# The last hidden group's down projection as seven block products for two output tiles at a time

## The chip, the cores and the metric

One program runs on one core of a Trainium2 chip. The metric is the device time of one execution in microseconds (us); lower is better. TensorE is called PE below, VectorE DVE, ScalarE ACT, GpSimd POOL; the queue on SyncE (SP) loads the weights.

## The reference

The reference is one step of a two-layer encoder trunk on 640 tokens (512 of a prompt, 8 streams of 16), width 1024, hidden width 2816, all in fp32:

```python
def half_swiglu(x, g, w_gu, w_down):
    h = rmsnorm(x, g) @ w_gu
    a, b = jnp.split(h, 2, axis=-1)
    return x + 0.5 * ((jax.nn.silu(a) * b) @ w_down)
...
def ple_add(x, p_i, g, w_gate, w_proj):
    gate = jax.nn.sigmoid((rmsnorm(x, g) @ w_gate).astype(F32))
    return x + (gate * (p_i @ w_proj).astype(F32)).astype(x.dtype)
```

Each layer is half_swiglu, a token mixer, half_swiglu, ple_add. The mixer is retention in layer 0 and stick-breaking attention in layer 1. So the eight phases are ffn, ret, ffn, ple, ffn, sb, ffn, ple, and each of the four ffn phases is followed by another phase that begins with an RMSNorm.

## The kernel before

x is kept transposed: 8 tiles x[:, d, :] of 128 features by 640 tokens. Every fp32 product is made of three passes in the reduced type fp32r: an operand is split into a high part (ACT copies it, names ending in _hi) and a low part (DVE subtracts, _lo), and PE multiplies hi*hi, hi*lo and lo*hi. The engines have one hand-written instruction order each and meet on counting semaphores; an engine waits at the head of its queue.

The weights come as a stream of slots. SP loads slot n into ring buffer raw[n % 4] as soon as the low part of slot n-4 has been made. In plain code ACT makes w_hi (split_hi, L1083) and DVE w_lo (split_lo, L1724), two slots ahead.

An ffn phase works the 22 hidden tiles in four groups, PIECES = (4, 6, 6, 6). Each group has its gate and up projection and then its down projection, which adds into x. Groups 1 to 3 do gate and up by a seven-product scheme over two-by-two blocks (winograd, product, L615) where plain blocks need eight. SEVEN_DOWN names the groups whose down projection also does that. There a job, d, makes two output tiles, d["out"] and d["out"] + 1, in 7 products of 9 matmuls (3 blocks, 3 passes, 320 columns): 63 matmuls. PE's order in such a job is product 1, product 3 of the job before, 2, 6, product 4 of the job before, 5, 7. The other engines serve it:

- ACT: snap1 (a copy within PSUM after product 1, L1184, needed by product 2), hi12 of the next job (L1147), snap2 (after product 6, needed by 7), hi34 (L1179, after the old job's product 4), hi56 and hi7 of the next job (L1167, L1173).
- DVE: c22 of the old job (L1856, needed by its product 4), lo56 (L1838, needed by product 6), lo7 (L1844), c11_c12 (L1873 and L1877, adds three quarters of the two tiles into x), the sums s1_s2 and s3 of the next job's weights (L1803 to L1809), c21 (L1883, the last quarter, which gives the PSUM banks free), lo12 of the next job (L1821), s4 (L1816) and lo34 (L1849).

The last group's down projection is plain before: for each of the 8 output tiles PE does 6 blocks in 3 passes over 2 halves, 36 matmuls (project, L544). After each tile, DVE adds it into x (L2052) and the next phase's operand is formed at once: ACT x_hi (feed_hi, L1087), ACT the square of x (square, L1094), DVE x_lo (feed_lo, L1729), POOL adds the square to ssum (add_squares, L1594 for the first, L1597 for the other seven). Two squares fit in the buffer, so square d waits for add d-2.

The next phase multiplies from the raw x and the gain and applies 1/rms afterwards. It begins so: ret runs its first projection (48 matmuls, q0) and then sum_squares (L567), which waits for all eight adds; sb does the same (its q0 starts only when the last down tile has left PSUM); ple runs three 12-matmul products of the small input p first (p_hi, p_lo, made during the down projection) and then sum_squares. p's fourth product waits for mean_square, the DVE reading of the sum. POOL issues the constants' DMAs of ret and sb after its last add.

Of the kernel before, what the change touches and what calls it, by code (L numbers as in the profile page):

```python
# [26 lines left out]
P = 128  # L27
D = 1024
KT = D // P
SEQ, STREAMS, STEP = 512, 8, 16  # L30
TOK = SEQ + STREAMS * STEP
# [18 lines left out]
SEVEN_DOWN = (1, 2)  # L50
# [153 lines left out]
def trunk(nc, phases, xT, pT, gains, wst, ones_d, ident_d, negtri_d, cs_d, dec_d, rmask_d, smask_d, gpow_d,  # L204
# [6 lines left out]
    with ctx:  # L211
# [221 lines left out]

        def g_tile(buf, k):

            return buf[:, k * TOK:(k + 1) * TOK]
# [99 lines left out]
        def _(pe):  # L536
# [45 lines left out]
            def ffn(c):  # L582
# [123 lines left out]
                for nf_at, nf in enumerate(PIECES):  # L706
# [363 lines left out]
        def _(act):  # L1070
# [19 lines left out]
            def square(c_fed, norm, d, s, value):  # L1090

                act.wait_ge(s, CREDIT + value)
                act.wait_ge(s_ssum, CREDIT + c_fed + d - 1)
                nc.scalar.activation(sq[:, d % 2, :], x[:, d, :], ACT.Square).then_inc(s_sq, 1)  # L1094
# [20 lines left out]
            def ffn(c):  # L1115
# [109 lines left out]

                def winograd(piece):
                    for old, d, new in jobs_of(c, piece):
# [25 lines left out]
                        if made:  # L1253
                            ghi(made)
                        if d["kind"] == "gu":
                            snap3(d)
                        if new:
                            hi56(new)
                            hi7(new)
                        else:  # L1260
                            act.wait_ge(s_prod[5], CREDIT + d["q"] + 1)
                            split_hi(c, d["m"], 0, 0, c["fill"] + d["m"])
                    if piece == LAST:
                        silu(d)
                        split_hi(c, d["m"] + 1, 0, 0, c["fill"] + d["m"] + 2)
                        ghi(d)

                for nf_at, nf in enumerate(PIECES):
# [38 lines left out]
                    for d in range(KT):  # L1307
                        if nf_at < LAST and d >= KT - 2:
                            if d == KT - 2:
                                first = fast_pairs(c, nf_at + 1)[0]  # L1310
                                hi12(first)
                                hi7(first)
                                hi56(first)
                            continue
                        split_hi(c, m + d, 0, 0, c["fill"] + m + d + 1)
                        if nf_at == LAST:
                            feed(c["fed"] + KT, c["norm"] + 1, d, s_free, o + m + d + 1)
                            if c["split_p"] and d == 4:
                                act.wait_ge(s_p, 16 * (c["ple"] + 1))
                                nc.scalar.activation(p_hi[:], p_raw[:], ACT.Copy).then_inc(s_phi, 1)  # L1320
# [263 lines left out]
        def _(pool):  # L1584
# [3 lines left out]
            def add_squares(fed, norm):  # L1588

                for d in range(KT - (norm == len(plan))):  # L1590
                    pool.wait_ge(s_sq, CREDIT + fed + d + 1)
                    if d == 0:
                        pool.wait_ge(s_ss, CREDIT + norm)
                        nc.gpsimd.tensor_copy(ssum[:], sq[:, 0, :]).then_inc(s_ssum, 1)  # L1594
                    else:
                        pool.wait_ge(s_ssum, CREDIT + fed + d)
                        nc.gpsimd.tensor_tensor(ssum[:], ssum[:], sq[:, d % 2, :], ALU.add).then_inc(s_ssum, 1)  # L1597
# [112 lines left out]
        def _(dve):  # L1710
# [46 lines left out]
            def ffn(c):  # L1757
# [177 lines left out]
                def winograd(piece):  # L1935
                    for old, d, new in jobs_of(c, piece):
# [20 lines left out]
                        if summed:  # L1957
                            c11_c12(summed)
                            s1_s2(new)
                            s3(new)  # L1960
                            c21(summed)
                            lo12(new)
                            s4(new)
                            lo34(d)
                            continue
# [20 lines left out]
                    if piece == LAST:  # L1986
                        c22(d)
                        split_lo(c, d["m"], 0, 0)
                        c12(d)
                        gated(d, 1)  # L1990
                        gated(d, 0)
                        split_lo(c, d["m"] + 1, 0, 0)
                        glo(d)

                for nf_at, nf in enumerate(PIECES):
# [52 lines left out]
                    for d in range(KT):  # L2048
# [4 lines left out]
                        if nf_at == LAST or d < KT - 2:  # L2053
# [3 lines left out]
                        if nf_at == LAST:  # L2057
                            feed_lo(c["fed"] + KT, c["norm"] + 1, d)
                            if c["split_p"] and d == 4:
                                dve.wait_ge(s_phi, CREDIT + c["ple"] + 1)  # L2060
                                tt(p_lo[:], p_raw[:], p_hi[:].bitcast(F), ALU.subtract).then_inc(s_plo, 1)
                        elif d == KT - 4:
# [597 lines left out]
```

## Time and profile before

| | us |
|---|---|
| median of three runs | 2795.7 |
| lowest and highest | 2793.03, 2796.23 |
| the profiled execution, its own time | 2792.98 |
| its span in the trace | 2791.4 |
| PE busy in the span | 2745.6 |
| DVE busy | 1918.0 |
| ACT busy | 1205.5 |

PE is busy nearly all the time; the other three matter only where PE has to wait for them. A time such as 308 ns of a matmul overlaps its neighbours; the distance from one matmul's start to the next is what counts.

### The profile page before, as it was taken

The page shows a single profiled execution, that of the slowest core. Times are in us where ns is not written, and L with a number is a line of the kernel's source. Part 1 is how long each engine was busy: PE and PEld are TensorE (multiplying, and loading weights), DVE is VectorE, ACT ScalarE, POOL GpSimd, SP SyncE. Part 2 cuts the span into 40 slices and gives each one's busy share as a digit, 9 for nine tenths or more (in the row PEclk, how much of TensorE's full clock was granted, in tenths as well). Part 3 has the DMA queues.
Part 4 walks back from the last instruction along what each step waited for, and adds up shares of the span by engine and source line. Part 5 has one row for each costly group of instructions (what it writes and reads, how often), then busy time and mean ns, then how long its engine had stood idle before and what let it go on. Part 6 is the DMA issues. An engine that isn't in the chain of part 4 may idle for free.

```text
span 2791.4 us, 47466 instructions
## 1 busy us (share of the span) xinstructions
PE 2745.6 (98%) x18946; PEld 2698.7 (97%) x18946; DVE 1918.0 (69%) x2687; ACT 1205.5 (43%) x1625; POOL 191.1 (7%) x190
## 2 busy tenths in 40 slices
PE   8999999999999999999999999999999999999997
PEld 8999999999999999999999999999999999999997
DVE  7788864646364677888657788864555567888755
ACT  5454443323232444454444454444434443545443
POOL 0000003101011110000010000002000020000021
PEclk9999999999999999999999999999999999999998
DMA  3322323333233313223321222323222112232231
GB/s 120 91 81 85 97 76 126 102 111 110 94 108 98 101 57 95 85 81 93 93 76 57 88 76 89 93 78 119 94 83 90 68 59 68 82 94 83 86 95 57
DMA packets 80908, 246.96 MB, mean 88 GB/s; under 512 B 8464, under 2 KB 25120, under 8 KB 79680
## 3 DMA queue, kind: packets, MB, share of 16 engines
q1 hardware_dynamic: 71408, 204.67, 23.5%
q0 software_dynamic: 9296, 39.40, 4.0%
q8 instruction: 149, 2.44, 0.4%
q14 instruction: 55, 0.45, 0.1%
HBM read 226.74 MB, written 17.30 MB: 87 GB/s over the span
## 4 chain that ended last, share of the span: by engine, by line
PE 94%; DVE 4%; ACT 1%; issue 1%; DMA 0%; ACTq 0%; SPq 0%; DVEq 0%
PE ps L615 42%; PE ps L544 32%; PE ps L927 7%; PE ps L803 4%; PE ps L980 2%; PE ps L596 1%; PE ps L901 1%; PE ps L1014 1%; DVE xn L1763 1%; PE ps L964 1%; PE ps L868 1%; PE ps L852 0%; PE ps L1000 0%; DVE w_lo L1724 0%; PE ps L871 0%
## 5 line engine op out<-in xcount | busy, mean ns | idle before, releaser
L1083 ACT ACTIVATE w_hi<-raw 128x1024 fp32r<-128x1024 f32 (+2 forms) x210 | 201.3, 959 | 516.6 <-PE ps L544 376.8
L1724 DVE TENSOR_TENSOR w_lo<-raw,w_hi 128x1024 fp32r<-128x1024 f32 (+2 forms) x210 | 236.8, 1128 | 93.9 <-ACT w_hi L1083 91.1
L544 PE MATMUL ps<-x_hi,w_hi 128*128 128x320 f32 x1216 | 284.3, 315 | 14.4 <-DVE x_lo L1729 8.9
L544 PE MATMUL ps<-x_lo,w_hi 128*128 128x320 f32 x1216 | 277.5, 309 | 0.0
L544 PE MATMUL ps<-x_hi,w_lo 128*128 128x320 f32 x1216 | 277.5, 310 | 0.0
L544 PEld LDWEIGHTS ps<-x_hi,w_hi 128*128 128x128 f32 x1216 | 203.9, 188 | 19.8 <-DVE w_lo L2466 8.9
L1147 ACT ACTIVATE wx_hi<-raw 128x1024 fp32r<-128x1024 f32 (+1 forms) x96 | 96.6, 1006 | 258.4 <-PE ps L615 226.2
L544 PEld LDWEIGHTS ps<-x_lo,w_hi 128*128 128x128 f32 x1216 | 203.8, 188 | 0.0
L544 PEld LDWEIGHTS ps<-x_hi,w_lo 128*128 128x128 f32 x1216 | 203.8, 188 | 0.0
L615 PE MATMUL ps<-x_hi,wx_hi 128*128 128x320 f32 x576 | 178.2, 309 | 3.0 <-DVE wx_lo L1821 3.0
L615 PE MATMUL ps<-x_hi,w_hi 128*128 128x320 f32 x576 | 178.7, 310 | 0.0
L615 PE MATMUL ps<-x_hi,w_lo 128*128 128x320 f32 x576 | 178.0, 309 | 0.0
L615 PE MATMUL ps<-x_lo,wx_hi 128*128 128x320 f32 x576 | 177.8, 309 | 0.0
L615 PE MATMUL ps<-x_lo,w_hi 128*128 128x320 f32 x576 | 177.6, 308 | 0.0
L615 PE MATMUL ps<-x_hi,wx_lo 128*128 128x320 f32 x576 | 177.5, 308 | 0.0
L615 PE MATMUL ps<-t_hi,w_lo 128*128 128x320 f32 x576 | 177.1, 307 | 0.0
L615 PE MATMUL ps<-t_lo,w_hi 128*128 128x320 f32 x576 | 177.1, 307 | 0.0
L615 PE MATMUL ps<-t_hi,w_hi 128*128 128x320 f32 x576 | 177.0, 307 | 0.0
L1821 DVE TENSOR_TENSOR wx_lo<-raw,wx_hi 128x1024 fp32r<-128x1024 f32 (+1 forms) x96 | 110.9, 1155 | 57.8 <-ACT wx_hi L1147 57.5
L544 PE MATMUL ps<-g_hi,w_hi 128*128 128x320 f32 x640 | 145.8, 308 | 0.0
L544 PE MATMUL ps<-g_hi,w_lo 128*128 128x320 f32 x640 | 145.5, 308 | 0.0
L544 PE MATMUL ps<-g_lo,w_hi 128*128 128x320 f32 x640 | 145.4, 308 | 0.0
(310 smaller groups left out, 7696.8 us busy)
## 6 DMA issues: line engine op xcount, KB each, us to landing
raw<-wst SPq DMA_DIRECT2D x292, 512.0 KB, 3.6
raw<-wst SPq DMA_DIRECT2D x96, 384.0 KB, 3.2
raw<-wst SPq DMA_DIRECT2D x32, 256.0 KB, 2.6
s<-st_d POOLq DMA_DIRECT2D x8, 1024.0 KB, 5.1
sts_o<-s POOLq DMA_DIRECT2D x16, 512.0 KB, 3.4
rd<-dec_d POOLq DMA_DIRECT2D x8, 640.0 KB, 5.6
kc<-kc_d POOLq DMA_DIRECT2D x8, 512.0 KB, 4.4
vc<-vc_d POOLq DMA_DIRECT2D x8, 512.0 KB, 5.2
```

The costliest lines, as they stand in the source:

```text
L544: last = nc.tensor.matmul(out[:, h, :], a, b[:, HALF * h:HALF * (h + 1)], start=start and q == 0, stop=stop and q == 2, skip_group_check=True)
L596: last = nc.tensor.matmul(acc(u)[:, h, :], a[:, p, w], b[:, k, cols], start=n in (0, 2) and k % 4 == 0 and q == 0, stop=n in (1, 3) and k ...
L615: last = nc.tensor.matmul(out, a[:, w], b[:, k, :], start=start and k == 0 and q == 0, stop=k == end - 1 and q == 2, skip_group_check=True)
L803: last = nc.tensor.matmul(out, a, b[:, p, w], start=part == 0 and k == 0 and q == 0 and t % 2 == 0, stop=part == 1 and k == 3 and q == 2, ...
L868: last = nc.tensor.matmul(f[:, t * DV:(t + 1) * DV], sc[:, t, :], vn[:, t, :], start=True, stop=t == 0)
L901: return nc.tensor.matmul(z[:, z0:z0 + w], bk[rows, par, b * P:(b + 1) * P], bq[rows, par, b * P:end], start=start, stop=False, skip_group ...
L927: last = nc.tensor.matmul(ps[:, sb_banks(use)[0], 0:HALF], a, b[:, xb, cols], start=n == 0 and q == 0, stop=n == len(blocks) - 1 and q == 2)
L980: last = nc.tensor.matmul(z[:, z0 + P * (b2 - b):z0 + ZW[b]], tri[:, int(b2 > b), :], src[:, from_piece, from_col:from_col + ZW[b2]], star ...
L1083: nc.scalar.activation(w_hi[:, (c["n"] + m) % 2, 0:cols], raw[:, r, 0:cols], ACT.Copy).then_inc(s_whi, 1)
L1147: nc.scalar.activation(wx_hi[:, 0:2, 0:d["width"]], raw_blocks(c, d)[:, 0:4:3, :], ACT.Copy).then_inc(s_hi12, 1)
L1724: tt(w_lo[:, p, 0:cols], raw[:, r, 0:cols], w_hi[:, p, 0:cols].bitcast(F), ALU.subtract).then_inc(s_wlo, 1)
L1821: tt(wx_lo[:, 0:2, w], raw_blocks(c, d)[:, 0:4:3, :], wx_hi[:, 0:2, w].bitcast(F), ALU.subtract).then_inc(s_lo12, 1)
```

## The change

The last group joins SEVEN_DOWN. Its down projection is then 4 jobs of 63 matmuls. The next phase's operand is formed two tiles at a time, in the middle of the following job (ACT fed, DVE two feed_lo). The squares come later: 0 and 1 in the third job, 2 to 4 at the end of the fourth, 5 to 7 after all of x_hi. The square buffers move to where the scheme's t_lo lies, since g_lo is in use to the end. Before a ple phase, the splitting of p sits in the third job. The gate values of the last group are formed with the extra sums of the seven-product layout (g_sum, ghi, glo), as in groups 1 and 2. Loads and slots keep their number and order.

```diff
--- before.py
+++ after.py
@@ -47,7 +47,7 @@
-SEVEN_DOWN = (1, 2)
+SEVEN_DOWN = (1, 2, 3)
...
@@ -251,6 +251,12 @@
+        with ExitStack() as s:
+
+            sb("over_t_hi2", [P, 3, 4, HALF], F, s)
+            sq_mix = sb("sq_mix", [P, 2, TOK], F, s)
+            sb("over_t_mid", [P, 3 * 4 * HALF - 4 * TOK], F, s)
+            sq_ple = sb("sq_ple", [P, 2, TOK], F, s)
...
@@ -471,7 +483,7 @@
-            nxt = fast_pairs(c, piece + 1)[0] if piece in SEVEN_DOWN else None
+            nxt = fast_pairs(c, piece + 1)[0] if piece < LAST else None
...
@@ -742,14 +754,6 @@
-                    if nf_at != LAST:
-                        m += KT
-                        continue
-                    with pe.Fori(0, KT // 4) as i:
-                        for j in range(4):
-                            step(m + j, i, 4)
-                            project(c, m + j, i, 4, (c["unit"] + 1 + m + j) % 4, [(k, k) for k in range(nf)],
-                                    tiles(g_hi), tiles(g_lo), ready if j == 0 else None)
...
@@ -1222,6 +1226,16 @@
+                def fed(d):
+
+                    act.wait_ge(s_up, CREDIT + 2 * d["sum"] + 2)
+                    feed_hi(c["norm"] + 1, d["out"])
+                    act.wait_ge(s_free, CREDIT + o + d["m"] + 2)
+                    feed_hi(c["norm"] + 1, d["out"] + 1)
+
+                def square_of(n):
+                    square(c["fed"] + KT, c["norm"] + 1, n, s_xhi, c["fed"] + KT + n + 1)
...
@@ -1252,6 +1266,14 @@
+                        if piece == LAST and d["kind"] == "dn":
+                            fed(old)
+                            if d["out"] == 4:
+                                square_of(0)
+                                square_of(1)
+                                if c["split_p"]:
+                                    act.wait_ge(s_p, 16 * (c["ple"] + 1))
+                                    nc.scalar.activation(p_hi[:], p_raw[:], ACT.Copy).then_inc(s_phi, 1)
...
@@ -1260,10 +1282,13 @@
                             split_hi(c, d["m"], 0, 0, c["fill"] + d["m"])
+                            for n in range(2, 5):
+                                square_of(n)
                     if piece == LAST:
-                        silu(d)
                         split_hi(c, d["m"] + 1, 0, 0, c["fill"] + d["m"] + 2)
-                        ghi(d)
+                        fed(d)
+                        for n in range(5, KT):
+                            square_of(n)
...
@@ -1956,12 +1976,20 @@
                             lo34(d)
+                            if piece == LAST and d["kind"] == "dn":
+                                feed_lo(c["fed"] + KT, c["norm"] + 1, summed["out"])
+                                feed_lo(c["fed"] + KT, c["norm"] + 1, summed["out"] + 1)
+                                if c["split_p"] and d["out"] == 4:
+                                    dve.wait_ge(s_phi, CREDIT + c["ple"] + 1)
+                                    tt(p_lo[:], p_raw[:], p_hi[:].bitcast(F), ALU.subtract).then_inc(s_plo, 1)
...
@@ -1986,11 +2014,11 @@
                     if piece == LAST:
                         c22(d)
                         split_lo(c, d["m"], 0, 0)
-                        c12(d)
-                        gated(d, 1)
-                        gated(d, 0)
+                        c11_c12(d)
+                        c21(d)
+                        feed_lo(c["fed"] + KT, c["norm"] + 1, d["out"])
                         split_lo(c, d["m"] + 1, 0, 0)
-                        glo(d)
+                        feed_lo(c["fed"] + KT, c["norm"] + 1, d["out"] + 1)
...
@@ -2050,16 +2078,11 @@
-                        if nf_at == LAST:
-                            feed_lo(c["fed"] + KT, c["norm"] + 1, d)
```

Three places in the engines' queues, all in the second ffn phase, ahead of a ple phase. Line numbers of the changed kernel are 4 higher on ACT and 20 higher on DVE.

ACT before, at the end of the down projection: from the square of tile 4 to the table load of the next phase. x_hi is the next operand, sq the square, p_hi the high part of p.

```order
L1087 ACTIVATE x_hi<-x,gain 128x640 [waits s_free]
L1094 ACTIVATE sq<-x 128x640 [waits s_ssum,s_free]
L1320 ACTIVATE p_hi<-p_raw 128x1280 [waits s_p]
L1083 ACTIVATE w_hi<-raw 128x768 [waits s_fill,s_raw3]
L1087 ACTIVATE x_hi<-x,gain 128x640 [waits s_free]
L1094 ACTIVATE sq<-x 128x640 [waits s_ssum,s_free]
L1083 ACTIVATE w_hi<-raw 128x1024 [waits s_fill,s_raw0]
L1087 ACTIVATE x_hi<-x,gain 128x640 [waits s_free]
L1094 ACTIVATE sq<-x 128x640 [waits s_ssum,s_free]
L1083 ACTIVATE w_hi<-raw 128x1024 [waits s_fill,s_raw1]
L1087 ACTIVATE x_hi<-x,gain 128x640 [waits s_free]
L1094 ACTIVATE sq<-x 128x640 [waits s_ssum,s_free]
```

ACT in the changed kernel, third job: from hi34 (w_hi<-raw) to the next job's snap1 (ps<-ps).

```order
L1183 ACTIVATE w_hi<-raw 128x2x384 [waits s_fill,s_sum4]
L1091 ACTIVATE x_hi<-x,gain 128x640 [waits s_up]
L1091 ACTIVATE x_hi<-x,gain 128x640 [waits s_free]
L1098 ACTIVATE sq_ple<-x 128x640 [waits s_ssum,s_xhi] x2
L1276 ACTIVATE p_hi<-p_raw 128x1280 [waits s_p]
L1171 ACTIVATE w_hi<-w_sum 128x2x384 [waits s_prod6,s_prod5,s_sum2]
L1177 ACTIVATE wx_hi<-raw 128x384 [waits s_prod7,s_sum3]
L1188 ACTIVATE ps<-ps 128x320 [waits s_prod1]
```

Between hi34 and hi56 (w_hi<-w_sum) stand now two x_hi, two squares and p_hi, all ahead of the snap1 that the fourth job's product 2 needs.

ACT in the changed kernel, end of the fourth job: from the x_hi of tile 4 to the table load.

```order
L1091 ACTIVATE x_hi<-x,gain 128x640 [waits s_up]
L1091 ACTIVATE x_hi<-x,gain 128x640 [waits s_free]
L1087 ACTIVATE w_hi<-raw 128x1024 [waits s_fill,s_raw0,s_prod5]
L1098 ACTIVATE sq_ple<-x 128x640 [waits s_ssum,s_xhi] x3
L1087 ACTIVATE w_hi<-raw 128x1024 [waits s_fill,s_raw1]
L1091 ACTIVATE x_hi<-x,gain 128x640 [waits s_up]
L1091 ACTIVATE x_hi<-x,gain 128x640 [waits s_free]
L1098 ACTIVATE sq_ple<-x 128x640 [waits s_ssum,s_xhi] x3
L1108 ACT_TABLE_LOAD
```

Three squares stand ahead of the second w_hi, and the last three behind both remaining x_hi; before, at most one square stood behind the last x_hi.

DVE in the changed kernel, third job: from s4 (raw<-raw,w_sum) to the end of c11_c12.

```order
L1841 TENSOR_TENSOR wx_lo<-raw,wx_hi 128x2x384 [waits s_hi12]
L1836 TENSOR_TENSOR raw<-raw,w_sum 128x384 [waits s_sum2,s_lo12]
L1869 TENSOR_TENSOR w_lo<-raw,w_hi 128x2x384 [waits s_whi]
L1749 SCALAR_TENSOR_TENSOR x_lo<-x,gain,x_hi 128x640 [waits s_xhi] x2
L1992 TENSOR_TENSOR p_lo<-p_raw,p_hi 128x1280 [waits s_phi]
L1876 SCALAR_TENSOR_TENSOR x<-ps,x 128x320 [waits s_prod7]
L1858 TENSOR_TENSOR w_lo<-w_sum,w_hi 128x2x384 [waits s_hi56]
L1864 TENSOR_TENSOR wx_lo<-raw,wx_hi 128x384 [waits s_whi]
L1893 SCALAR_TENSOR_TENSOR x<-ps,x 128x640 [waits s_prod3]
L1897 SCALAR_TENSOR_TENSOR x<-ps,x 128x2x320 [waits s_c22,s_up]
```

The two x_lo and p_lo stand ahead of c22 and lo56 (w_lo<-w_sum,w_hi).

## Rows read from the trace of the kernel before

**Rows 1.** The page's head: span, and busy time of each engine

```profile
span 2791.4 us, 47466 instructions
...
PE 2745.6 (98%) x18946; PEld 2698.7 (97%) x18946; DVE 1918.0 (69%) x2687; ACT 1205.5 (43%) x1625; POOL 191.1 (7%) x190
```

**Rows 2.** The chain that ended last, in order: start, us, what

```profile
726.51 2.69 issue
729.20 15.92 PE ps L803 x119
...
865.52 14.40 PE ps L803 x120
...
1870.65 42.25 PE ps L544 x288
```

**Rows 3.** Windows: us, busy of PE, PEld, DVE, ACT, POOL; granted clock; DMA

```profile
729.20:735.00 5.80, 5.80 (x37) 5.80 (x37) 0.00 (x0) 0.00 (x0) 0.00 (x0) 0.71 0.10 40
```

**Rows 4.** PE's waits, whole span: us in total, times, longest

```profile
PE ps L615 <- ACT ps L1192: 1.3, 8, 0.2
...
PE ps L927 <- DVE x L2052: 0.9, 1, 0.9
```

**Rows 5.** Timeline of DVE in group 2's third down job, first ffn: start, us

```profile
307.75 0.49 DVE L1883 SCALAR_TENSOR_TENSOR x<-ps,x 128x320 f32<-128x320 f32 x1 [0.82 <-PE ps L615]
...
309.62 0.95 DVE L1849 TENSOR_TENSOR w_lo<-raw,w_hi 128x768 fp32r<-128x768 f32 x1
310.49 0.48 DVE L1856 SCALAR_TENSOR_TENSOR x<-ps,x 128x320 f32<-128x320 f32 x1
310.89 0.95 DVE L1838 TENSOR_TENSOR w_lo<-w_sum,w_hi 128x768 fp32r<-128x768 f32 x1
...
312.96 0.82 DVE L1873 SCALAR_TENSOR_TENSOR x<-ps,x 128x640 f32<-128x640 f32 x1 [0.66 <-PE ps L615]
313.82 0.82 DVE L1877 SCALAR_TENSOR_TENSOR x<-ps,x 128x640 f32<-128x640 f32 x1
```

**Rows 6.** Timeline of ACT in the same job

```profile
307.74 0.84 ACT L1179 ACTIVATE w_hi<-raw 128x768 fp32r<-128x768 f32 x1 [0.96 <-PE ps L615]
309.05 0.85 ACT L1167 ACTIVATE w_hi<-w_sum 128x768 fp32r<-128x768 f32 x1 [0.47 <-PE ps L615]
310.38 0.53 ACT L1173 ACTIVATE wx_hi<-raw 128x384 fp32r<-128x384 f32 x1 [0.48 <-PE ps L615]
311.64 0.42 ACT L1184 ACTIVATE ps<-ps 128x320 f32<-128x320 f32 x1 [0.74 <-PE ps L615]
```

**Rows 7.** Timeline of DVE in the last group, second ffn

```profile
1399.51 1.98 DVE L2061 TENSOR_TENSOR p_lo<-p_raw,p_hi 128x1280 fp32r<-128x1280 f32 x1 [0.82 <-ACT p_hi L1320]
...
1412.98 1.22 DVE L1724 TENSOR_TENSOR w_lo<-raw,w_hi 128x1024 fp32r<-128x1024 f32 x1 [0.33 <-ACT w_hi L1083]
1414.13 0.88 DVE L1729 SCALAR_TENSOR_TENSOR x_lo<-x,gain,x_hi 128x640 fp32r<-128x640 f32 x1
```

**Rows 8.** Timeline of ACT in the last group, second ffn

```profile
1398.21 1.26 ACT L1320 ACTIVATE p_hi<-p_raw 128x1280 fp32r<-128x1280 f32 x1
...
1411.89 1.06 ACT L1083 ACTIVATE w_hi<-raw 128x1024 fp32r<-128x1024 f32 x1 [2.87 <-PE ps L544]
1412.86 0.81 ACT L1087 ACTIVATE x_hi<-x,gain 128x640 fp32r<-128x640 f32 x1
1413.58 0.72 ACT L1094 ACTIVATE sq<-x 128x640 f32<-128x640 f32 x1
```

**Rows 9.** Timeline of POOL: an add beside the last group, four back to back

```profile
1414.38 2.05 POOL L1597 TENSOR_TENSOR ssum<-ssum,sq 128x640 f32<-128x640 f32 x1 [3.23 <-ACT sq L1094]
...
2279.11 7.20 POOL L1597 TENSOR_TENSOR ssum<-ssum,sq 128x640 f32<-128x640 f32 x4 [6.99 <-ACT sq L1094]
```

**Rows 10.** The instructions that use ssum: count, shortest, median and longest in ns

```profile
L1597 POOL TENSOR_TENSOR ssum<-ssum,sq x55: 1576/1721/2593, 409.0 to 2770.6; 128x640 f32<-128x640 f32 x55
```

More of the change, by code:

```diff
@@ L432, in b_side, with squares @@
             return quarter(whole, *at_x[product]) if product < 5 else extra[:, product - 5, :, :]
+        def squares(norm):
+            if norm == 0 or norm > len(phases) - 1 or phases[norm - 1] != "ffn":
+                return sq
+            return sq_ple if phases[norm] == "ple" else sq_mix
         def g_tile(buf, k):
@@ L1093, in square @@
                 act.wait_ge(s_ssum, CREDIT + c_fed + d - 1)
-                nc.scalar.activation(sq[:, d % 2, :], x[:, d, :], ACT.Square).then_inc(s_sq, 1)
+                nc.scalar.activation(squares(norm)[:, d % 2, :], x[:, d, :], ACT.Square).then_inc(s_sq, 1)
             def feed(c_fed, norm, d, s, value):
@@ L1307, in ffn @@
                     for d in range(KT):
-                        if nf_at < LAST and d >= KT - 2:
+                        if d >= KT - 2:
                             if d == KT - 2:
@@ L1315, in ffn @@
                         split_hi(c, m + d, 0, 0, c["fill"] + m + d + 1)
-                        if nf_at == LAST:
[L1317 to L1320, printed above, removed]
                     m += KT
@@ L1593, in add_squares @@
                         pool.wait_ge(s_ss, CREDIT + norm)
-                        nc.gpsimd.tensor_copy(ssum[:], sq[:, 0, :]).then_inc(s_ssum, 1)
+                        nc.gpsimd.tensor_copy(ssum[:], squares(norm)[:, 0, :]).then_inc(s_ssum, 1)
                     else:
                         pool.wait_ge(s_ssum, CREDIT + fed + d)
-                        nc.gpsimd.tensor_tensor(ssum[:], ssum[:], sq[:, d % 2, :], ALU.add).then_inc(s_ssum, 1)
+                        nc.gpsimd.tensor_tensor(ssum[:], ssum[:], squares(norm)[:, d % 2, :], ALU.add).then_inc(s_ssum, 1)
             def ffn(c):
@@ L1958, in winograd @@
                             c11_c12(summed)
-                            s1_s2(new)
-                            s3(new)
+                            if new:
+                                s1_s2(new)
+                                s3(new)
                             c21(summed)
-                            lo12(new)
-                            s4(new)
+                            if new:
+                                lo12(new)
+                                s4(new)
                             lo34(d)
+                            if piece == LAST and d["kind"] == "dn":
[4 more added lines that the diff above has]
+                                    tt(p_lo[:], p_raw[:], p_hi[:].bitcast(F), ALU.subtract).then_inc(s_plo, 1)
                             continue
@@ L2052, in ffn @@
                         stt(out=xd, in0=acc(u), scalar=0.5, in1=xd, op0=ALU.mult, op1=ALU.add).then_inc(s_free, 1)
-                        if nf_at == LAST or d < KT - 2:
+                        if d < KT - 2:
                             split_lo(c, m + d, 0, 0)
@@ L2056, in ffn @@
                             t_low(3 + d, 6 + d)
-                        if nf_at == LAST:
-                            feed_lo(c["fed"] + KT, c["norm"] + 1, d)
[L2059 to L2062, printed above, removed]
+                        if d == KT - 4:
                             first = fast_pairs(c, nf_at + 1)[0]
```

## The prediction

> **What bounds the kernel now.** I read the page's head first: PE is busy in 98% of the span, DVE in 69%, ACT in 43% [rows 1]. So only PE's own work and the places where PE stands count. The chain in order gives PE's pace: the 288 matmuls of the last group's down projection take 42.25 us, 0.1467 us from one to the next [rows 2]. The 308 ns of a single matmul overlap and must not be summed. The list of PE's waits says how the seven-product scheme runs today: in the 8 down projections that use it PE stands 1.3 us in all, before product 7 (ACT's snap2) [rows 4]. So group 1 and 2's down projection is fed in time. The question is whether the last group's is too, since it has more to feed: the next phase's operand, the squares and p.
>
> **What the change removes.** 8 tiles of 36 matmuls become 4 jobs of 63, so 36 fewer in each ffn and 144 in the kernel: 144 x 0.1467 = 21.1 us. All of it is on PE, and would be the gain if PE never stood longer.
>
> **What it adds before the third job ends.** The first two jobs have room, since they carry at most two x_hi and two x_lo more. At the first, PE stands for snap2 as in groups 1 and 2: 1.3/8 = 0.16 us [rows 4], four times 0.65.
>
> The third job can be laid over group 2's [rows 5, 6]. There, hi34 starts at 307.74 and the fourth job's snap1 at 311.64, 0.20 after product 1's last matmul has gone out (311.44). Product 3 takes 9 x 0.1467 = 1.32, so product 2 wants snap1 at 312.76. On ACT, the next operation starts about 0.1 before the end of the last (1412.86 to 1413.58 for an x_hi of 0.81 [rows 8]). The changed queue is then: hi34 to 308.48, two x_hi of 0.73 to 309.94, two squares of 0.62 to 311.18, p_hi (1.26 long [rows 8]) to 312.34, hi56 0.75, hi7 0.43, and snap1 of 0.42 ends at 313.94. Ahead of ple PE stands 1.2 us. Without p_hi snap1 ends at 312.78: 0.05.
>
> On DVE, lo34 gives way at 310.49 [rows 5]. Two x_lo (0.88 long, 0.80 apart [rows 7]) go to 312.09. p_lo waits for p_hi (312.44) and takes 1.98 [rows 7], to 314.38. c22 takes 0.40 and lo56 0.95, which ends at 315.73. Product 6 is due 1.32 after product 2 could start (313.98), at 315.30: 0.4 more. Ahead of ret and sb, lo56 ends at 313.44 and product 6 is due at 314.1: nothing. So ple pays 1.6, twice 3.2; ret and sb 0.1 together. The third job is tight, by less than one operation.
>
> **The end of the down projection.** Call T the time when the last product 4 has gone out. From the old job's product 4 to the last one lie three products, 3.96. DVE has in that time hi34 to wait for (0.22 + 0.84), lo34 0.87, two x_lo 1.60 and c22 0.48, some 4.1 with the handing over: PE stands 0.14 in each ffn, 0.56. Then come the next phase's w_lo (1.22 [rows 7]), c11_c12 (0.86 and 0.74 apart [rows 5]) and c21 (0.49), which ends at T+1.8. Before, PE stood 0.9 for this at sb [rows 4]; now 1.8. ret and ple need it only for their second unit. At ple that is 0.07, twice.
>
> ACT after the fourth job's hi34: two x_hi, w_hi (1.06), squares 2, 3, 4, w_hi, x_hi 6, x_hi 7, squares 5, 6, 7. Square 4 waits for add 2. An add takes 1.80 when they follow each other (7.20 for four [rows 9]), and add 2 cannot start before square 2, T-1.3, so it ends at T+0.5. From there square 4, w_hi and the two x_hi go to T+3.6, square 5 to T+4.3, and adds 5, 6 and 7 with 1.84 each to T+9.8. Before, a single add stood behind the last square: the square ended at 1414.30 and the add at 1416.43 [rows 8, 9].
>
> What PE does until it asks for the sum: ret 48 matmuls, T+7.04, so it stands 2.85. ple 36 matmuls and the 0.07, T+5.35: 4.5, twice 9.1. sb starts at T+1.8, and the eighth block of its first half is due at T+4.9. Its x_lo comes behind x_lo 6 and the second w_lo at T+5.8: 0.95. It then asks at T+9.8, when the sum is there: 0.05. ret's eighth block is due at T+6.16, behind that x_lo.
>
> Sum of what is added: 0.65 + 0.1 + 3.2 + 0.56 + 0.14 + (0.9 + 0.95 + 0.05) for sb + 2.85 + 9.1 = 18.5. With the 21.1 that leaves 2.6 us gained: ret and sb win 2 to 3 each, each ple loses about 1.3.
>
> **What is costed at nothing.** The extra work for the seven-product gate values on DVE (sums of four blocks of 320 columns and the low parts of three more for each two hidden tiles) lie beside 24.6 us of matmuls for two jobs, as in groups 1 and 2, where PE has no other wait. PE's code grows by the unrolled loop; groups 1 and 2 are unrolled and show no idle time. POOL issues the constants of ret and sb behind the last add, some 5 us later against PE's clock than now. PE's first use of them is behind two projections of 7.04, so I take that as hidden; without that cover it would cost up to 2 us at each, the part of the 5 us that PE has not itself stood.
>
> **TensorE's clock.** After the 2.69 us in which PE stood at 726.51, 119 matmuls took 15.92 us where the same work takes 14.40 [rows 2], and the granted clock of that stretch was 0.71 [rows 3], a mixture of 2.4 and 1.2 GHz. So a stand of that length cost 1.5 us more. The ple stands are longer (4.5) and ret's as long (2.85). At all three it would be 4.5, at none 0. I take 2.0, since one row is all that shows it. That leaves 0.6 us gained.
>
> The Trainium skill, "TensorE: Matmul & The Clock Gate", Part 1, says that an idle array falls to half its clock and gets it back after sustained work. The trace agrees at 729 us with its 0.71. By that rule alone all three stands would pay, and the sum would be a loss of 1.9 us.
>
> **The add's price.** The row of all 55 adds has 1.58, 1.72 and 2.59 us [rows 10]. The one beside x_lo took 2.05 [rows 7, 9]. Five adds (2, 3 or 4, then 5 to 7) stand in the chain to T+9.8, so at 2.05 each seam is 1.25 later, 5 us in all. At 1.72 it is 1.6 us less in all. I keep 1.80, the row of a run of adds.
>
> The Trainium skill, "GPSIMD Engine Reference", section 8, says that GpSimd shares its SBUF interfaces with DVE and contends with DVE instructions that read two SBUF inputs, as w_lo and x_lo do. It speaks for 2.05 beside DVE; at the tail DVE is idle after T+5.8. By the rule for all adds the sum would be a loss of 4.4 us.
>
> **Rivals.** (A) The sum of squares does not hold PE. Speaks for it: POOL is busy in only 7%, and today it never holds PE here. Against it: three squares stand behind the last x_hi, and three adds behind those. Without the 12.0 us of these waits, and so without the clock's 2.0, the gain is 2.6 + 12.0 = 14.6: 2781.1. It decides from 5 us less wait. (B) The adds run at the slow end, near 2.59, while DVE works beside them: 0.79 more for five adds at four seams, 15.8, so 2810.9. It ends slower from about 2.11 us an add (6.2/20 more). Against it: the median is 1.72. (C) The third job's backlog does not resolve in the fourth, because DVE and ACT have each slipped by a whole product, 1.32, at all four seams: 5.3 us, 2800.4. It is inside my range. (D) The change removes fewer products than it says: PE's list of instructions rules it out.
>
> **How the numbers follow.** The profiled execution took 2792.98, with 1.6 outside its span; 0.6 less is 2792.4. The median of three is 2795.7, 2.7 higher, and against that the forecast is 2795.1, which I round to 2795. From no change this measurement tells 0.2%, 5.6 us: faster is below 2790.1, slower above 2801.3. The forecast, a balance of 21.1 against about 20, has 0.70 with (C) in it; its own range is from 2791 (adds at 1.72, no loss of clock) to 2802 (adds at 2.05, clock at all three). (A) has 0.12 and its half-way forms 0.05; (B) 0.13. The range of 2789 to 2802 holds the forecast's and a little of (A).
>
> **What the profile would show.** The down projection of the last group in about 37.3 us ahead of ret and sb and 38.9 ahead of ple instead of 42.25. PE waiting for POOL's ssum before sum_squares, 4.5 us at both ple and 2.9 at ret, none or little at sb. Adds 5 to 7 back to back. PE waiting 1.2 us for the PSUM copy of ACT in ple's fourth job. A granted clock under 1 behind the ple waits. The prediction is wrong if PE asks for the sum and finds it there, or if the waits sit in the jobs instead.

## The result and the profile after

The changed kernel takes 2812.09 us (median of four runs, 2810.98 to 2812.99) against 2794.36 for the kernel before on the same chip (2792.55 to 2796.23): a ratio of 1.0061, with a 95% interval of 1.0049 to 1.0074, so 17.7 us slower. Forecast was 2795 with a range of 2789 to 2802. The profiled execution took 2810.98.

The page's head after, which answers to [rows 1]:

```profile
span 2809.4 us, 47590 instructions
...
PE 2740.1 (98%) x18802; PEld 2685.5 (96%) x18802; DVE 2036.0 (72%) x2867; ACT 1245.4 (44%) x1705; POOL 194.6 (7%) x190
```

The 144 matmuls are gone (18946 to 18802), yet PE's busy time fell by 5.5 us only, where they were worth 21.1: the rest of PE's work took longer. PE's waits after, whole span (us in total, times, longest), which answer to [rows 4]:

```profile
PE ps L579 <- POOL ssum L1617: 11.6, 2, 5.8
PE ps L556 <- DVE x_lo L1749: 11.6, 2, 8.2
PE ps L931 <- DVE x_lo L1749: 4.5, 2, 3.9
...
PE ps L627 <- DVE w_lo L1858: 3.1, 4, 1.1
...
PE ps L627 <- ACT ps L1188: 2.3, 2, 1.1
...
PE ps L627 <- ACT ps L1196: 2.0, 12, 0.2
...
PE ps L931 <- DVE x L1903: 1.5, 1, 1.5
```

The 8.2 in the second row is the start of the program; the other 3.4 stand in ret's first projection. So 5.8 for the sum at each ple, 3.4 for x_lo at ret, 4.5 for x_lo and 1.5 for x at sb. The sum at ple was foreseen; the x_lo waits were not, except for 0.95 at sb. At ret the forecast had a stand of 2.85 for the sum, and none is there: PE comes to it late, after the stand for x_lo.

The reason shows in the engines' timelines of the second ffn's end. The last product has gone out at 1408.0 (T): product 4's first matmul starts at 1406.56 and nine take 1.32, with a tenth of handing over. DVE from the third job's x_lo on:

```profile
1393.46 2.14 DVE L1749 SCALAR_TENSOR_TENSOR x_lo<-x,gain,x_hi 128x640 fp32r<-128x640 f32 x2
1395.52 2.83 DVE L1992 TENSOR_TENSOR p_lo<-p_raw,p_hi 128x1280 fp32r<-128x1280 f32 x1
...
1406.42 1.22 DVE L1744 TENSOR_TENSOR w_lo<-raw,w_hi 128x1024 fp32r<-128x1024 f32 x1
...
1411.62 1.61 DVE L1749 SCALAR_TENSOR_TENSOR x_lo<-x,gain,x_hi 128x640 fp32r<-128x640 f32 x1 [1.99 <-ACT x_hi L1091]
1413.15 2.56 DVE L1744 TENSOR_TENSOR w_lo<-raw,w_hi 128x1024 fp32r<-128x1024 f32 x1
1415.63 2.15 DVE L1749 SCALAR_TENSOR_TENSOR x_lo<-x,gain,x_hi 128x640 fp32r<-128x640 f32 x1
```

and POOL's adds:

```profile
1395.07 1.93 POOL L1617 TENSOR_TENSOR ssum<-ssum,sq_ple 128x640 f32<-128x640 f32 x1 [0.15 <-POOL ssum L1614]
1406.62 5.92 POOL L1617 TENSOR_TENSOR ssum<-ssum,sq_ple 128x640 f32<-128x640 f32 x3 [9.62 <-ACT sq_ple L1098]
1413.01 6.16 POOL L1617 TENSOR_TENSOR ssum<-ssum,sq_ple 128x640 f32<-128x640 f32 x3 [0.47 <-ACT sq_ple L1098]
```

The w_lo at 1413.15, which starts 0.14 behind an add, takes 2.56 where it had 1.22 [rows 7], and the x_lo behind it 2.15 where it had 0.88. The w_lo at 1406.42 starts 0.20 ahead of an add and keeps its 1.22; that add is the one that is long, 2.47 against 1.6 for the two behind it. The last three adds take 6.16 instead of the 5.5 of the sum, and end at T+11.2 instead of T+9.8.

The third reading is the clock. The chain from the second ffn's ple on:

```profile
1419.31 2.47 PE ps L579 x4
1422.75 63.88 PE ps L556 x420
```

Behind it the windows say how that went (the columns are those of [rows 3]); the third is at sb:

```profile
1419.30:1422.75 3.45, 2.48 (x5) 1.19 (x5) 0.93 (x2) 0.07 (x1) 0.00 (x0) 0.50 0.00 0
1422.75:1432.00 9.25, 9.25 (x49) 9.25 (x50) 7.99 (x10) 2.55 (x3) 0.00 (x0) 0.76 0.17 58
...
1924.55:1931.85 7.30, 7.30 (x33) 6.98 (x34) 0.33 (x2) 2.52 (x3) 5.00 (x8) 0.70 0.67 223
```

The granted clock is 0.50, that is 1.2 GHz, directly behind the 5.8 us stand, and only a part of the next 9.25 us has 2.4 GHz. The 420 matmuls that follow would take 61.6 at the pace of [rows 2] and take 63.88.

A seam is the passage from an ffn's last down projection into the next phase. Points that both chains share say what each seam cost. The changed kernel falls behind by 1.5 us over ret, 7.4 over the first ple, 4.0 over sb and 6.6 over the second ple, 19.5 in all, with 5.28 us of matmuls removed at each. So the change adds 6.8, 12.7, 9.3 and 11.9, together 40.6, where the forecast had 20.5 (18.5 and 2.0 for the clock). The own times of the profiled executions differ by 18.0 (2810.98 and 2792.98). The 1.5 between lie elsewhere: the changed kernel gains 3.6 at the stand of [rows 2] at 726.51, which was 0.6 long in this execution, and loses 1.7 near 2266 and 0.4 before the first seam.

### The profile page after: what moved, and what is told of

Its sections match the earlier page's. It is cut to its first block, busy times and chain, and to the rows that moved or that the text cites. A ratio compares the mean times of both kernels' runs of the same rounds, so it can differ in the third digit from the quotient of the medians.

```text
span 2809.4 us, 47590 instructions
## 1 busy us (share of the span) xinstructions
PE 2740.1 (98%) x18802; PEld 2685.5 (96%) x18802; DVE 2036.0 (72%) x2867; ACT 1245.4 (44%) x1705; POOL 194.6 (7%) x190
## 4 chain that ended last, share of the span: by engine, by line
PE 90%; DVE 6%; ACT 2%; issue 1%; POOL 1%; DMA 0%; ACTq 0%; SPq 0%; DVEq 0%; POOLq 0%
PE ps L627 44%; PE ps L556 26%; PE ps L931 7%; PE ps L807 4%; PE ps L984 2%; PE ps L608 1%; DVE x_lo L1749 1%; POOL ssum L1617 1%; PE ps L905 1%; PE ps L1018 1%; DVE xn L1783 1%; PE ps L968 1%; DVE w_lo L1744 1%; ACT w_hi L1087 1%; PE ps L872 1%
## 5 line engine op out<-in xcount | busy, mean ns | idle before, releaser
L1087 ACT ACTIVATE w_hi<-raw 128x1024 fp32r<-128x1024 f32 (+1 forms) x178 | 174.2, 979 | 416.6 <-PE ps L556 283.6
L1744 DVE TENSOR_TENSOR w_lo<-raw,w_hi 128x1024 fp32r<-128x1024 f32 (+1 forms) x178 | 214.7, 1206 | 82.9 <-ACT w_hi L1087 82.5
L1151 ACT ACTIVATE wx_hi<-raw 128x1024 fp32r<-128x1024 f32 (+1 forms) x108 | 106.8, 989 | 287.6 <-PE ps L627 256.1
L627 PE MATMUL ps<-g_hi,w_hi 128*128 128x320 f32 x576 | 178.0, 309 | 3.2 <-DVE w_lo L1858 3.1
L627 PE MATMUL ps<-g_hi,w_lo 128*128 128x320 f32 x576 | 177.1, 308 | 0.0
L627 PE MATMUL ps<-g_lo,w_hi 128*128 128x320 f32 x576 | 177.1, 308 | 0.0
L1841 DVE TENSOR_TENSOR wx_lo<-raw,wx_hi 128x1024 fp32r<-128x1024 f32 (+1 forms) x108 | 122.3, 1132 | 66.1 <-ACT wx_hi L1151 66.1
```

The source lines that it names most:

```text
L627: last = nc.tensor.matmul(out, a[:, w], b[:, k, :], start=start and k == 0 and q == 0, stop=k == end - 1 and q == 2, skip_group_check=True)
L1087: nc.scalar.activation(w_hi[:, (c["n"] + m) % 2, 0:cols], raw[:, r, 0:cols], ACT.Copy).then_inc(s_whi, 1)
L1151: nc.scalar.activation(wx_hi[:, 0:2, 0:d["width"]], raw_blocks(c, d)[:, 0:4:3, :], ACT.Copy).then_inc(s_hi12, 1)
L1744: tt(w_lo[:, p, 0:cols], raw[:, r, 0:cols], w_hi[:, p, 0:cols].bitcast(F), ALU.subtract).then_inc(s_wlo, 1)
L1841: tt(wx_lo[:, 0:2, w], raw_blocks(c, d)[:, 0:4:3, :], wx_hi[:, 0:2, w].bitcast(F), ALU.subtract).then_inc(s_lo12, 1)
```

## The experiments

The times of before on the chips of the experiments were 2793.79, 2795.26 and 2794.61 (medians).

**The adds made short.** POOL's adds touch 8 columns each, and so does its copy of the first square, which the expectation below leaves whole. The sum is incomplete.

```diff
+    w = slice(0, 8 if is_mix(norm) else TOK)
-    nc.gpsimd.tensor_copy(ssum[:], squares(norm)[:, 0, :]).then_inc(s_ssum, 1)
+    nc.gpsimd.tensor_copy(ssum[:, w], squares(norm)[:, 0, w]).then_inc(s_ssum, 1)
...
-    nc.gpsimd.tensor_tensor(ssum[:], ssum[:], squares(norm)[:, d % 2, :], ALU.add)
+    nc.gpsimd.tensor_tensor(ssum[:, w], ssum[:, w], squares(norm)[:, d % 2, w], ALU.add)
```

> The changed kernel, but at the four norms behind an ffn phase POOL's adds of the squares after the first touch only 8 of the 640 columns each, with all waits and semaphores kept (the first copy stays whole; the sum of squares is then incomplete). Theory 1 (POOL's full adds are the cause, in two ways: PE waits for the last of them, and DVE's w_lo and x_lo take about twice as long while an add runs beside them): w_lo of 1024 columns back to 1.22 us and x_lo to 0.88 in the seams, lo56 in the third job back to 0.95, no wait for ssum (now 5.8 at each ple), none for x_lo at ret (3.4), little at sb (4.5), and no half-speed matmuls behind them; about 30 us less than the changed kernel's 2812, so 2778 to 2784. Rival (the operand formed two tiles at a time is itself late, whatever POOL does): the x_lo waits at ret and sb stay, only the two ssum waits go, 2795 to 2800.

Measured: 2777.74, ratio 0.9942 (0.9925 to 0.9958), 34.3 less than the changed kernel and 0.3 below the range expected. No wait for ssum or x_lo is left but that of the start. DVE at ret's seam:

```profile
436.26 0.89 DVE L1755 SCALAR_TENSOR_TENSOR x_lo<-x,gain,x_hi 128x640 fp32r<-128x640 f32 x1 [0.60 <-ACT x_hi L1095]
437.07 1.22 DVE L1750 TENSOR_TENSOR w_lo<-raw,w_hi 128x1024 fp32r<-128x1024 f32 x1
438.20 0.88 DVE L1755 SCALAR_TENSOR_TENSOR x_lo<-x,gain,x_hi 128x640 fp32r<-128x640 f32 x1
```

The same queue, in the same order, runs at its old durations. Theory 1 holds and the rival falls: the operand formed two tiles at a time is not late by itself.

**The sum of the first square.** PE no longer waits for the adds, but they run. PE multiplies a copy of the first square, so the mean is that of one square.

```diff
-    pe.wait_ge(s_ssum, CREDIT + c["fed"] + KT)
+    pe.wait_ge(s_ssum, CREDIT + c["fed"] + (1 if mix else KT))
```

> The changed kernel, but at the four norms behind an ffn phase PE multiplies a copy of the first square (it is put into rstd's place), so that it waits for the first square alone; the seven adds run as before beside DVE, and nothing of PE's waits for them (the mean is that of one square; DVE waits for the adds before its fifth copy of ple's p products and before sb's 1/rms). It keeps the slowing of DVE and takes the wait for the sum away. Theory 1: the x_lo waits of ret (3.4) and sb (4.5) stay with their half-speed matmuls, both ple seams gain 5.8 of wait and some 3 of clock: about 2795. Rival (DVE isn't really slowed by adds, the x_lo waits come from something that depends on the sum): they go too, 2780 to 2785. If the clock costs nothing, 2800.

Measured: 2801.68, ratio 1.0031 (1.0019 to 1.0044). PE's waits:

```profile
PE ps L560 <- DVE x_lo L1756: 11.8, 2, 8.4
PE ps L560 <- issue: 8.1, 2, 4.1
PE ps L937 <- DVE x_lo L1756: 4.5, 2, 3.9
```

The x_lo waits at ret and sb stay to a tenth (3.4 beside the start's 8.4, and 4.5), so they don't hang on the wait for the sum. The time is 6.7 us above the expectation, and the second row says where: p's fourth product stands 4.1 at each ple where it had stood 1.0, 6.2 more in all. It waits for mean_square, and DVE's timeline at the first ple has that behind x_lo 7:

```profile
1411.02 2.56 DVE L1751 TENSOR_TENSOR w_lo<-raw,w_hi 128x1024 fp32r<-128x1024 f32 x1
1413.51 2.15 DVE L1756 SCALAR_TENSOR_TENSOR x_lo<-x,gain,x_hi 128x640 fp32r<-128x640 f32 x1
1415.58 0.81 DVE L1762 TENSOR_SCALAR scr<-ps 128x640 f32<-128x640 f32 x1
```

So two chains end almost together at ple, the adds and DVE's own queue, which the adds stretch. Taking PE's wait for the sum away uncovers the other.

**PE kept busy.** Spare matmuls fill the long waits.

```diff
+    def keep_busy(c, count):
+        for n in range(count):
+            nc.tensor.matmul(acc(c["ss"])[:, n % 2, :], w_hi[:, 0, 0:P], ...)
```

> The changed kernel with spare matmuls of 320 columns (into the bank that the sum overwrites) ahead of the three kinds of long wait: 38 ahead of each ple sum, 22 ahead of ret's eighth block and 25 ahead of sb's, which last a little less than the waits do today. The waits' ends stay where they are. Theory 2 (a large part of the loss is the granted clock behind the waits: 0.50 to 0.87 in those stretches, some 1.5 us at ret, 2.3 at sb, 2.5 to 3.3 at each ple beyond what the same matmuls take at full clock): 8 to 10 us less, 2802 to 2804. Rival (the clock isn't what makes them slow, or it falls anyway): no change, 2812.

Measured: 2802.77, ratio 1.0031 (1.0018 to 1.0044), 9.3 less than the changed kernel although PE does 123 matmuls more. The window behind the first ple's sum:

```profile
1418.00:1430.00 12.00, 10.75 (x68) 9.87 (x67) 9.63 (x13) 2.65 (x4) 0.48 (x1) 1.00 0.13 42
```

Here the clock stays at 1.00, where it was 0.50. So the clock behind the waits costs some 9.3 us of the changed kernel's time, about half of the 17.7 it lost.

**Late squares with the plain down projection.** The kernel before, with only the squares moved.

```diff
-    feed(c["fed"] + KT, c["norm"] + 1, d, s_free, o + m + d + 1)
+    act.wait_ge(s_free, CREDIT + o + m + d + 1)
+    feed_hi(c["norm"] + 1, d)
+    for n in {5: (0, 1), 6: (2, 3, 4), 7: (5, 6, 7)}.get(d, ()):
+        square(c["fed"] + KT, c["norm"] + 1, n, s_free, o + m + n + 1)
```

> The kernel before, with its plain down projection, but with ACT's squares as late as in the changed kernel: squares 0 and 1 behind x_hi 5, squares 2 to 4 behind x_hi 6, squares 5 to 7 behind x_hi 7. Theory 1: the chain of adds behind the last x_hi sets the end. Adds 5 to 7 end about 8.1 us after the last down product has gone out; PE asks for the sum 7.0 after it at ret and 5.3 at ple. So about 1 at ret, 2.8 and some clock at each ple, nothing at sb: 2800 to 2807. Rival (late squares alone do no harm, the two-tile order of the operand does): 2794 to 2796.

Measured: 2816.48, ratio 1.008 (1.0063 to 1.0097). That is more than the changed kernel, without one matmul removed. Its waits and, from its chain, the adds at the first ple:

```profile
PE ps L567 <- POOL ssum L1600: 11.5, 4, 4.2
```

```profile
1414.02 2.07 POOL ssum L1600
1416.22 1.60 POOL ssum L1600
1417.95 2.62 POOL ssum L1600
1420.70 1.96 POOL ssum L1600
1422.79 1.54 POOL ssum L1600
1424.47 1.54 POOL ssum L1600
1426.14 2.47 PE ps L567 x4
```

Six adds take 12.0 us; alone behind each other they take 1.54 to 1.60, the ones beside w_lo or x_lo 1.96 to 2.62. The rival falls. The expectation was too low in part for that reason, and in part because it had only "some clock": PE's waits for the sum are 11.5 of the 22.7 us lost, and the granted clock in the 3.5 us behind the first ple's wait is again 0.50. So late squares with whole adds are enough for such a loss, without the seven products.

**Squares spread over the jobs.**

```diff
-    if d["out"] == 4:
-        square_of(0)
-        square_of(1)
+    square_of(d["out"] - 2)
+    square_of(d["out"] - 1)
```

> The changed kernel with the squares earlier: squares 0 and 1 in the second job (behind x_hi 0 and 1), 2 and 3 in the third, 4 and 5 in the fourth ahead of the next w_hi, 6 and 7 behind x_hi 7. Only two adds are left for the tail. Theory 1a (the number of adds behind the last product sets the loss): the ssum waits at ple fall from 5.8 to 2 to 3, the x_lo waits at ret and sb from 3.4 and 4.5 to about 1, half of the clock's 10 us goes: 2796 to 2802, with some 0.5 us more in each of the second and fourth jobs, as POOL's adds now run beside DVE's lo56 there too. Rival (the lateness comes with the two-tile operand, not with the squares): above 2808.

Measured: 2808.8, ratio 1.0051 (1.0034 to 1.0067), 3.3 less than the changed kernel. The waits:

```profile
PE ps L631 <- DVE w_lo L1860: 10.7, 8, 2.3
...
PE ps L583 <- POOL ssum L1619: 5.0, 3, 2.3
```

The ssum wait fell to 2.3 as expected, but lo56 now holds product 6 up in 8 places, 10.7 us in all, where the changed kernel had 3.1. The expectation had 0.5 for each such job. Moving the adds earlier moves their damage into the jobs, where DVE has no room. The time is outside the 2796 to 2802 of theory 1a and where its rival had it, above 2808; but the lateness still stands beside adds, and the short adds, which keep the two-tile operand, have none of it. So how late the squares come is not the whole cause: wherever whole adds run beside DVE's work they cost about as much.

**Spare work on POOL, in the kernel before.**

```diff
+    for n in range(14):
+        nc.gpsimd.tensor_tensor(ssum[:], ssum[:], rstd[:], ALU.add)    # a copy in the second ffn
```

> The kernel before with spare work on POOL, 14 instructions of 128x640 each one behind the other: adds (ssum<-ssum,rstd) beside group 2's down projection in the first ffn, copies (ssum<-rstd) at the same place in the second, adds beside group 3's gate and up in the third, nothing in the fourth; each result is overwritten before it is used. By itself it prices a neighbour on POOL. Theory 1: beside adds DVE's instructions with two SBUF operands take about twice as long (w_lo of 768 columns 1.9 instead of 0.95, x sums from PSUM unchanged at 0.82), and PE waits in group 2's down projection by several us; beside copies less. An add itself takes 1.5 alone and 2.0 to 2.6 beside such an instruction. Rival (POOL's neighbour costs DVE nothing and the long instructions in the seams were waits for something else): DVE as in the fourth ffn, and the time of before.

Measured: 2823.0, ratio 1.0099 (1.0079 to 1.0119). DVE's groups beside the adds, first ffn, 283 to 312 us (busy, mean ns):

```profile
L1821 DVE TENSOR_TENSOR raw<-raw 128x384 f32<-128x384 f32 x1 | 1.9, 1912 | 0.0
...
L1889 DVE SCALAR_TENSOR_TENSOR x<-ps,x 128x640 f32<-128x640 f32 x1 | 0.8, 824 | 0.0
L1885 DVE SCALAR_TENSOR_TENSOR x<-ps,x 128x640 f32<-128x640 f32 x1 | 0.8, 812 | 0.0
```

The same line beside copies in the second ffn (1273.5 to 1288 us), and without a neighbour in the fourth:

```profile
L1821 DVE TENSOR_TENSOR raw<-raw 128x384 f32<-128x384 f32 x1 | 1.1, 1067 | 0.0
...
L1821 DVE TENSOR_TENSOR raw<-raw 128x384 f32<-128x384 f32 x3 | 1.7, 551 | 0.0
```

So 0.55 us alone, 1.07 beside a copy, 1.91 beside an add; 0.82 for the sum from PSUM in each case. No wait of PE names POOL, and the spare work costs the kernel 27.7 us. The rival falls.

**The sum on PE.** No adds; each square has a tile and PE sums them in the reduced type.

```diff
+    for d in range(KT):
+        pe.wait_ge(s_sq, CREDIT + c["fed"] + d + 1)
+        for h in range(2):
+            last = nc.tensor.matmul(acc(u)[:, h, :], ones_r[:],
+                                    sq8(c["norm"], d)[:, HALF * h:HALF * (h + 1)], start=d == 0, ...)
```

> The changed kernel with ACT's squares in the same places, but POOL adds nothing at the four norms behind an ffn phase: ACT writes each square in the reduced type into a tile of its own (eight tiles: in y_hi and y_lo ahead of ret and sb, in t_lo and wx_hi ahead of ple) and PE sums them with 16 matmuls of 320 columns against ones, where it had two fp32 ones of 1.08 us together. Theory 1 (adds are the cause): as with the short adds, 2777.7, plus 4 times (16 x 0.1467 - 1.08) = 5.1, so 2781 to 2785. Rival (the short adds helped because their semaphores came early, and a full sum in time isn't to be had): PE waits for the last square instead, 2 to 3 us at each ple, 2790.

Measured: 2795.32, ratio 1.0001 (0.9992 to 1.0011). PE's first wait is the difference:

```profile
PE ps L570 <- DVE x_lo L1783: 19.4, 1, 19.4
```

The copy of the ones at the head of ACT's queue waited for their load, and the first x_hi stood behind it, 11.0 us longer than with the short adds (8.4). The kernels below make that copy later.

**The sum on PE, queue moved.** p later, two squares instead of three last in the queue, x_hi 6 and 7 ahead of the second w_hi, x_lo 4 to 7 behind c21.

```diff
     c21(d)
-    feed_lo(c["fed"] + KT, c["norm"] + 1, d["out"])
+    for n in range(d["out"] - 2, KT):
+        feed_lo(c["fed"] + KT, c["norm"] + 1, n)
     split_lo(c, d["m"] + 1, 0, 0)
-    feed_lo(c["fed"] + KT, c["norm"] + 1, d["out"] + 1)
```

> As the sum on PE, with the rest of the queue moved as well: p_hi behind the fourth job's snap1 on ACT and p_lo behind its c11_c12 on DVE (third job before), squares 0 to 2 behind that snap1, 3 to 5 behind the next phase's first w_hi, 6 and 7 last; both x_hi 6 and 7 ahead of the second w_hi; x_lo 4 to 7 behind the last c21 and ahead of the second w_lo. Theory: the third job's stands at ple (1.1 for snap1, with its clock nothing) go, sb's wait for c21 falls from 1.5 to near 0, and product 4 of the last job no longer waits for c22: 4 to 5 us under the sum on PE, 2776 to 2780. Rival (x_lo 4 to 7 are then late for the first projection): no better than the sum on PE, with x_lo waits at sb.

Measured: 2790.77, ratio 0.9987 (0.9977 to 0.9996), 4.6 under the sum on PE, with the same late start (a first wait of 20.6), which neither expectation had. The snap1 stands are gone; sb's wait for c21 was 1.4, since w_hi stood behind x_hi 4 and 5.

**The two again, the copy of the ones made later.** The moved one also has the next phase's first w_hi ahead of x_hi 4 and 5, and its w_lo ahead of c22.

```diff
+    if c["i"] == 0 and nf_at == 1:
+        act.wait_ge(s_const, 32)
+        nc.scalar.activation(ones_r[:], ones[:], ACT.Copy).then_inc(s_ones, 1)
```

> As the sum on PE, but the rounded copy of the ones is made in the first ffn phase's second group, where it was made at the very start and held the start up (PE's first wait for x_lo was 19.4 us against 8.4 with the short adds). Theory 1 as before: 2795.3 - 11.0 = 2784.3, so 2782 to 2786. Rival (something besides the start took the gain): above 2790.

Measured: 2784.34, ratio 0.9963 (0.995 to 0.9977), as expected. With the first wait back at 8.3 the start is accounted for.

> As the moved queue with the sum on PE, with the copy of the ones in the second group too, and at the end of the last job the next phase's first w_hi ahead of x_hi 4 and 5, its w_lo ahead of c22. By its first wait of 20.6 against 8.4: 2790.8 - 12.2 = 2778.6, and 0.4 less at sb (its stand for c21 1.4 to 0.9): 2776 to 2780, faster than the kernel before by some 16 us. Rival: it stays within 0.2% of the kernel before.

Measured: 2780.88, ratio 0.995 (0.9936 to 0.9963): 13.7 us faster than the kernel before and 31.2 faster than the changed one. Its waits behind the start:

```profile
PE ps L651 <- ACT ps L1223: 2.0, 12, 0.2
...
PE ps L651 <- DVE x L1911: 0.7, 4, 0.2
...
PE ps L955 <- DVE x L1938: 0.7, 1, 0.7
```

It is 0.9 us above the range expected. The 2.33 us of the sum's matmuls at each seam instead of 1.08 are 5.0 of what still lacks to the 21.1; a version that also keeps that was not tried.

**The sum on PE with the plain down projection.** The same edit in the kernel before.

> The kernel before, with its plain down projection and squares where they were, and the sum of squares on PE as in the two kernels above. Theory 1 (today's adds cost PE nothing there, so PE only gets 4 times 1.27 us of matmuls more): 2797 to 2801, so that the seven products and not the sum are what gains. Rival (the adds cost the kernel before time as well, by DVE, and taking them away is the whole gain): 2780 to 2790.

Measured: 2795.05, ratio 1.0003 (0.9994 to 1.0012). The rival falls: taking the adds away gains nothing by itself. It is 2 us below the range expected. In its profiled execution the stand of [rows 2] at 726.51 is missing, worth 4.3 us: ahead of it this kernel is 1.1 us behind the kernel before, and behind it 3.2 ahead. Whether that comes from the edit wasn't tried. Against this kernel the seven products with the same sum gain 10.7 us unmoved and 14.2 moved.

**Only the splitting of p later.**

```diff
     snap1(d)
+    if piece == LAST and d["kind"] == "dn" and d["last"] and c["split_p"]:
+        act.wait_ge(s_p, 16 * (c["ple"] + 1))
+        nc.scalar.activation(p_hi[:], p_raw[:], ACT.Copy).then_inc(s_phi, 1)
```

> The changed kernel with only the splitting of p moved, p_hi behind the fourth job's snap1 and p_lo behind its c11_c12. The third job's stands at ple (1.1 for snap1, 1.1 for lo56) should fall to 0 and 0.5 as ahead of ret; the last product then goes out 1.7 us sooner at each ple, and the adds with it: 3.4 us less than the changed kernel's 2812, 2807 to 2810. Rival (p_lo only moves the lateness into the fourth job, where w_lo and c22 come late, slower still beside the first two adds): no change.

Measured: 2808.25, ratio 1.0051 (1.0036 to 1.0067), 3.8 less than the changed kernel, as expected: the snap1 stands are gone, and lo56 holds PE up by 1.9 in all where it was 3.1.

## Why the prediction was wrong

Two steps failed. The working made POOL's adds dear beside DVE and left DVE's own instructions at their undisturbed lengths, so it had no stand for x_lo at ret and 0.95 at sb; they were 3.4 and 4.5. And it put 2.0 us on the clock, which cost about 9.3. The matmuls removed, 21.1 us, were right: the count fell by 144, and of the 40.6 us that the seams added, 19.5 were left as loss. Term by term:

- First job, snap2 at 0.16: as the list of waits has it (2.0 for 12 in all, where 1.3 was for 8). But the list leaves a part out. The first two matmuls of product 7 start 0.47 and 0.22 behind the one in front, not 0.1467, so the stand costs PE 0.40. It is so at each stand, some 0.25 more, and comes to about 1.0 at each seam.
- Third job, snap1 ahead of ple at 1.2: about right (1.13 in the list). lo56 was put at 0.4 ahead of ple and nothing at ret and sb. It was 1.08 and 0.47. Product 6 was late because DVE's instructions ran beside the first copy and add: two x_lo took 2.14 instead of 1.68 everywhere, then ahead of ple p_lo 2.83 instead of 1.98, and ahead of ret and sb lo56 1.93 instead of 0.95.
- The last job's c22 at 0.14 was 0.28, by the distance of the starts. sb's c21 held PE 1.5 instead of 1.8. The last down projection lasts about 38.6 us (252 x 0.1467 and 1.6 of gaps) ahead of ret and 40.4 ahead of ple, instead of 37.3 and 38.9.
- The squares and adds of the tail: their order was right, add 2 starts at T-1.35 (T-1.3 foreseen), add 5 at T+5.0 instead of T+4.3, the last ends at T+11.2 instead of T+9.8. PE stood 5.8 instead of 4.5 at each ple. (The 2.85 and 4.5 of the sum belong to an end at T+9.9; from T+9.8 they would be 2.8 and 4.45.)
- x_lo 7 at T+5.8: the first of the two steps. It ended at T+9.8 at ret (444.65, with T at 434.82). Of the 4.0 us, 0.7 and 1.4 and 1.3 are x_lo 6, w_lo and x_lo 7 themselves, the rest the later x_hi. So ret's eighth block stood 3.4, and sb's blocks 0.6 and 3.9 where 0.95 was foreseen. At ret it cost little more than the sum would have: the adds ended at 446.05, against PE's asking at 446.46.
- The clock at 2.0 of a possible 4.5: the second step, and the larger one. It was sized on one stand of 2.69 us that cost 1.5. Kept busy, PE gained 9.3. Behind the stand of 5.8 the clock was 0.50, the fp32 sum and the next products ran at it, and sb, to which the forecast gave no stand of the kind, paid as well.

Of the 20.1 us between 40.6 and 20.5, the clock is 7.3, the parts of the stands that the list leaves out about 3, x_lo at sb and ret 3.5 and 0.6, the sum at ple 2.5, and lo56 2.3; the rest is small terms.

**The add's price** had the contention in it, but on one side only. "DVE is idle after T+5.8" was the working's reason to take a row of adds as undisturbed. DVE was made late by those adds, so it wasn't idle, and each slowed the other. Nor was the row of adds that gave 1.80 undisturbed: its four took 2.00, 1.58, 1.58 and 1.60, and the 2.00 is the one beside a w_lo (2278.44 to 2279.67). Alone, an add was 1.6 and 0.1 to the next. Rival (B) was the right place and nearly the right time, 2810.9 to 2812.1, with a chance of 0.13; its mechanism was half of it. It put 15.8 us on PE's wait for slow adds, whereas that wait grew by 2.6 us at the two ples and the rest is DVE's lateness and the clock. Its number is luck to that extent. Rival (A)'s time, 2781.1, is near what the kernel takes once the adds are short or gone (2777.7 with short ones; with a whole sum on PE 2784.3, and 2780.9 with the queue moved), but (A) itself, that the adds run and hold nobody, is refuted.

The rule quoted from the Trainium skill, "GPSIMD Engine Reference", section 8, names contention with DVE instructions that read two SBUF inputs. The spare work on POOL agrees: 0.55 becomes 1.91 us beside an add, and the sum with a PSUM operand keeps 0.82. In the prediction the rule was used to price the adds (2.05) and not DVE's own instructions, where it bit harder.

## What to carry to other kernels

When work is moved next to another engine's work, price the neighbours on both sides: first look in the trace for a pair of that kind side by side, then lengthen both. A chain behind the last product (here squares and adds) counts in full, for what was spread over the work before has nothing to hide behind; try the late chain on the old kernel first, which here lost 22.7 us by itself. And a stand of PE costs more than its length, since here the granted clock was halved behind the long ones.

## What the runs showed of the hardware

- Instructions of DVE with two SBUF operands and POOL's adds of 128x640 seem to take turns. A 384-column instruction of 0.55 us took 1.07 beside copies of 1.05 on average and 1.91 beside adds of 1.86, so its own time and half to three quarters of the neighbour's. In the changed kernel w_lo, started 0.14 us behind an add, took 1.34 longer than alone; started 0.20 ahead of one it took no longer, and the add took 2.47 instead of 1.6. That they take turns is read from durations and starts; no run isolates it.
- Instructions of DVE with an operand in PSUM did not change: 0.82 in each case.
- After 5.8 us without work PE's granted clock was 0.50, throughout the 3.45 us window of the sum. With spare matmuls in the same place it was 1.00.
- Sixteen matmuls in the reduced type, which sum eight tiles, took 2.33 us; the fp32 ones that sum one tile took 1.08 (four records, 0.27 from start to start). They replace 28 adds and 4 copies on POOL.
